# An expert mixture with its unseen first expert in a 64-slot pass, its sorting done ahead of the passes, and its low halves laid over the raw blocks

## The reference, cut to what matters

```python
def swiglu(h, wg, wu, wd):
    return (jax.nn.silu(h @ wg) * (h @ wu)) @ wd

def moe_swiglu(h, router, wg, wu, wd):
    t = h.reshape(B_ * S_, D_)
    logits = (t @ router).astype(jnp.float32)
    top_v, top_i = lax.top_k(logits, TOP_K)
    gates = jax.nn.softmax(top_v, axis=-1)
    gate_full = jnp.sum(jax.nn.one_hot(top_i, N_EXPERTS, dtype=jnp.float32) * gates[..., None], axis=1)
    out = jnp.zeros_like(t)
    for e in range(N_EXPERTS):
        out = out + gate_full[:, e:e + 1].astype(t.dtype) * swiglu(t, wg[e], wu[e], wd[e])
    return out.reshape(B_, S_, D_)
```

## Time and profile before

| | us |
|---|---|
| median of 3 runs | 3103.74 (3100.64 to 3104.61) |
| the profiled execution | 3096.48 |
| its span | 3094.7 |
| TensorE busy | 2879.8 (93%) |
| VectorE busy | 2287.9 (74%) |
| ScalarE busy | 1651.6 (53%) |
| transfers | 739.29 MB, mean 239 GB/s |
| mean granted TensorE clock | 0.969 |

### The profile page before, as it was taken

How to read it: one execution, slowest core, us unless ns; L and a number is a source line. 1 busy time by engine, 2 the same in 40 slices (tenths; PEclk the granted TensorE clock), 3 DMA queues, 4 the chain that set the end, 5 groups by cost and what they waited for, 6 DMA issues and landing times. The chain is left out here.

```text
span 3094.7 us, 49251 instructions
## 1 busy us (share of the span) xinstructions
PE 2879.8 (93%) x17960; PEld 2375.9 (77%) x17961; DVE 2287.9 (74%) x3284; ACT 1651.6 (53%) x1865; POOL 72.3 (2%) x75
## 2 busy tenths in 40 slices
PE   7999898999999999989889988879998998999988
PEld 3796546898888999977769976668877877888776
DVE  5675754889788666666655567668889889888988
ACT  4354303335534344346344354357778778777886
POOL 0000000000000000000000000000000100000010
PEclk9999899999999999999889999879999999999999
DMA  8570232455687666633145331289999999999997
GB/s 310 204 253 30 106 146 91 144 164 186 257 257 238 201 214 210 213 130 127 57 150 183 122 129 38 107 345 373 364 374 419 397 371 419 394 373 379 390 408 284
DMA packets 228491, 739.29 MB, mean 239 GB/s; under 512 B 23831, under 2 KB 60104, under 8 KB 225480
## 3 DMA queue, kind: packets, MB, share of 16 engines
q1 hardware_dynamic: 222648, 704.49, 62.0%
q0 software_dynamic: 5360, 31.98, 3.1%
q10 hardware_dynamic: 288, 0.26, 0.0%
HBM read 707.28 MB, written 29.36 MB: 238 GB/s over the span
## 5 line engine op out<-in xcount | busy, mean ns | idle before, releaser
L3942 DVE TENSOR_TENSOR moe_lo<-moe_raw,moe_hi 128x2048 fp32r<-128x2048 f32 (+1 forms) x397 | 860.0, 2191 | 125.3 <-ACT moe_hi L3745 123.5
L3745 ACT ACTIVATE moe_hi<-moe_raw 128x2048 fp32r<-128x2048 f32 (+1 forms) x397 | 724.0, 1838 | 245.5 <-PE moe_pB L3611 105.2
L3611 PE MATMUL moe_pB<-moe_hi,moe_hEh 128*128 128x512 f32 x560 | 223.9, 400 | 7.0 <-DVE moe_hEl L4121 5.7
L3611 PE MATMUL moe_pB<-moe_lo,moe_hEh 128*128 128x512 f32 x560 | 220.1, 393 | 0.0
L3611 PE MATMUL moe_pB<-moe_hi,moe_hEl 128*128 128x512 f32 x560 | 219.9, 393 | 0.0
L1971 PE MATMUL exp_pO<-exp_vh,exp_ah 128*128 128x512 f32 x512 | 200.1, 391 | 1.8 <-DVE exp_al L2056 1.8
L1971 PE MATMUL exp_pO<-exp_vl,exp_ah 128*128 128x512 f32 x512 | 200.0, 391 | 0.0
L3623 PE MATMUL moe_pB<-moe_hi,moe_hEh 128*128 128x512 f32 x448 | 182.7, 408 | 18.4 <-DVE moe_lo L3942 17.8
L1971 PE MATMUL exp_pO<-exp_vh,exp_al 128*128 128x512 f32 x512 | 199.2, 389 | 0.0
L1996 ACT ACTIVATE exp_vh<-value_ring 128x1024 fp32r<-128x1024 f32 x128 | 134.8, 1056 | 103.4 <-PE exp_pO L1971 81.5
L2045 DVE TENSOR_TENSOR exp_vl<-value_ring,exp_vh 128x1024 fp32r<-128x1024 f32 x128 | 156.4, 1222 | 30.6 <-ACT exp_vh L1996 28.6
(11 more groups left out here) (861 smaller groups left out, 7268.0 us busy)
## 6 DMA issues: line engine op xcount, KB each, us to landing
moe_raw<-in_moe_w SPq DMA_DIRECT2D x758, 512.0 KB, 7.7
value_ring<-in_peer_v SPq DMA_DIRECT2D x128, 512.0 KB, 4.4
key_ring<-in_peer_u SPq DMA_DIRECT2D x64, 512.0 KB, 3.6
exp_us<-in_peer_u SPq DMA_DIRECT2D x64, 512.0 KB, 5.1
inp_w<-in_w_mod SPq DMA_DIRECT2D x48, 512.0 KB, 7.5
inp_w<-in_w_tiles SPq DMA_DIRECT2D x40, 512.0 KB, 6.2
gates<-route_big POOLq DMA_DIRECT2D x8, 2048.0 KB, 7.2
exp_gs<-gates SPq DMA_DIRECT2D x32, 512.0 KB, 5.7
```

What stands on the lines that cost most here:

```text
L3611: i = pe.matmul(pB[:, kind], l[:, kd], m[:, n % HALVES, ns], start=kd == 0 and x == 0, stop=kd == KD - 1 and x == 2)
L3745: act.activation(hi[:, n % HALVES:n % HALVES + count_], raw[:, n % RING:n % RING + count_], ACT.Copy).then_inc(hi_ready, count_)
L3942: dve.tensor_tensor(lo[:, n % HALVES:n % HALVES + count_], raw[:, n % RING:n % RING + count_], hi[:, n % HALVES:n % HALVES + count_], ALU. ...
```

## The change

- WIDE, RANKS: pass 0 becomes narrow. The order is narrow, wide, wide, narrow, wide, narrow, wide, narrow, and the wide passes keep ranks 1 to 4. EXTRA goes from 4 to 5.
- The ring `lo` is gone. The low halves are written over the raw blocks: `low` is a second, fp32r tensor at the address of `raw`, 21 slots. The ring `hi` has HIGH = 12 slots in place of 6 (the sum of the tiles stays 33 blocks).
- A raw slot is loaded again when TensorE has used the block in it (`used`), not when VectorE has lowered it; the first 21 loads wait for nothing.
- The first three conversions (EARLY = 3, six blocks) of ScalarE and VectorE stand ahead of pass 0; in pass 0 ScalarE waits for `used` only from the 13th block on.
- `tables` stands ahead of the counts, `ranks` and `sorted_passes` among the first three low operations; PREPARE of what is left is gates after 5, extras after 9, extra_slots after 15, and a new part, extra_gates (the gates of the extra passes, until now the end of `gates`), after 19. Scratch for the sorting moves to the tile hrow.
- The split of the first tokens is the narrow one, 64 slots a bank.

```diff
-    WIDE = (True, True, False, True, False, True, True, False)
-    RANKS = (0, 1, 5, 2, 6, 3, 4, 7)
-    EXTRA = 4
+    WIDE = (False, True, True, False, True, False, True, False)
+    RANKS = (0, 1, 2, 5, 3, 6, 4, 7)
+    EXTRA = 5
...
-    RING, HALVES, PRE = 21, 6, 2
+    RING, HIGH, PRE, EARLY = 21, 12, 2, 3
...
-        both = n % RING < RING - 1 and n % HALVES < HALVES - 1
+        both = n % RING < RING - 1 and n % HIGH < HIGH - 1
...
+    def first_turn(t):
+        return isinstance(t.at, int) and t.at == 0
...
-        hi, lo = sb("hi", [P, HALVES, D], F32R), sb("lo", [P, HALVES, D], F32R)
+        low = nc.alloc_sbuf_tensor_at("moe_low", [P, RING, D], F32R, offset=nc.sbuf_base - RING * D * 4)
+        hi = sb("hi", [P, HIGH, D], F32R)
...
-        AHEAD_LO, AHEAD_USED = RING, HALVES
+        AHEAD_USED = HIGH
...
-                    sp.wait_ge(lo_ready, t.at * PASS + n + 1)
+                    if not first_turn(t) or n >= RING:
+                        sp.wait_ge(used, t.at * PASS + (n + 1 + HIGH - RING))
                     sp.dma_start(raw[:, n % RING], ...).then_inc(raw_loaded[n % RING], 16)
...
-                    pe.wait_ge(lo_ready, AHEAD_LO + t.at * PASS + n + 1)
+                    pe.wait_ge(lo_ready, t.at * PASS + (n + 1))
...
-                            for x, m in enumerate((hi, lo)):
-                                i = pe.matmul(pB[:, kind], hEh[:, kd], m[:, n % HALVES, ns], ...)
+                            for x, m in enumerate((high_of(n), low[:, n % RING])):
+                                i = pe.matmul(pB[:, kind], hEh[:, kd], m[:, ns], ...)
...
-                    act.wait_ge(used, t.at * PASS + n + count_)
-                    act.activation(hi[:, n % HALVES:n % HALVES + count_], raw[...], ACT.Copy).then_inc(hi_ready, count_)
+                    if not first_turn(t) or n + count_ > HIGH:
+                        act.wait_ge(used, t.at * PASS + (n + count_))
+                    act.activation(hi[:, n % HIGH:n % HIGH + count_], raw[...], ACT.Copy).then_inc(hi_ready, count_)

                 high(fixed[0], SPANS[0])
                 act.wait_ge(d_ready, 1)
                 act.activation(e[:], df[:], ACT.Exp).then_inc(e_ready, 1)
+                for span in SPANS[1:EARLY]:
+                    high(fixed[0], span)
...
-                PREPARE = {4: tables, 6: ranks, 8: sorted_passes, 10: extras, 12: extra_slots, 14: gates}
+                tables()
+                dve.wait_ge(rank_psum, 1)
...
+                def lower(t, span):
+                    n, count_ = span
+                    dve.wait_ge(hi_ready, t.at * PASS + n + count_)
+                    dve.tensor_tensor(low[:, n % RING:n % RING + count_], raw[:, n % RING:n % RING + count_], hi[:, n % HIGH:n % HIGH + count_], ALU.subtract).then_inc(lo_ready, count_)
+
+                lower(fixed[0], SPANS[0])
+                ranks()
+                for span in SPANS[1:EARLY]:
+                    lower(fixed[0], span)
+                sorted_passes()
+
+                PREPARE = {5: gates, 9: extras, 15: extra_slots, 19: extra_gates}
...
-                dve.tensor_tensor(hEl[:, 0:KD // 2]..., pX[:, 0], hEh[:, 0:KD // 2]..., ALU.subtract)
+                for h, ready in enumerate((half_ready, hEh_ready)):
+                    ks = slice(h * KD // 2, (h + 1) * KD // 2)
+                    dve.wait_ge(ready, 1)
+                    i = dve.tensor_tensor(hEh[:, ks, HALF:P], pX[:, h]...[:, :, 0:HALF], hEh[:, ks, 0:HALF], ALU.subtract)
+                i.then_inc(h_ready, 1)
```

More of the change, by code:

```diff
@@ L3609, in wide_product @@
                             ns, kd = slice(b * BANK, (b + 1) * BANK), 2 * u + b
-                            for x, (l, m) in enumerate(((hEh, hi), (hEh, lo), (hEl, hi))):
-                                i = pe.matmul(pB[:, kind], l[:, kd], m[:, n % HALVES, ns], start=kd == 0 and x == 0, stop=kd == KD - 1 and x == 2)
+                            for x, (l, m) in enumerate(((hEh, high_of(n)), (hEh, low[:, n % RING]), (hEl, high_of(n)))):
+                                i = pe.matmul(pB[:, kind], l[:, kd], m[:, ns], start=kd == 0 and x == 0, stop=kd == KD - 1 and x == 2)
                         i.then_inc(used, 1)
@@ L3651, in wide_down @@
                             hs = slice(h * BANK, (h + 1) * BANK)
-                            for x, (l, m) in enumerate(((ah, hi), (ah, lo), (al, hi))):
-                                i = pe.matmul(pY[:, h], l[:, u], m[:, n % HALVES, hs], start=g == 0 and u == 0 and x == 0,
+                            for x, (l, m) in enumerate(((ah, high_of(n)), (ah, low[:, n % RING]), (al, high_of(n)))):
+                                i = pe.matmul(pY[:, h], l[:, u], m[:, hs], start=g == 0 and u == 0 and x == 0,
                                               stop=g == GROUPS - 1 and u == UNITS - 1 and x == 2)
@@ L3664, in narrow_down @@
                             hs = slice(h * BANK, (h + 1) * BANK)
-                            for x, m in enumerate((hi, lo)):
-                                i = pe.matmul(pY[:, h], both[:, u], m[:, n % HALVES, hs], start=g == 0 and u == 0 and x == 0,
+                            for x, m in enumerate((high_of(n), low[:, n % RING])):
+                                i = pe.matmul(pY[:, h], both[:, u], m[:, hs], start=g == 0 and u == 0 and x == 0,
                                               stop=g == GROUPS - 1 and u == UNITS - 1 and x == 1)
@@ L3811, in narrow @@
                             narrow_silu(t, last)
-                        high(t, span)
+                        if s >= EARLY or not first_turn(t):
+                            high(t, span)
                         if s == behind_block(UNITS):
@@ L4020, in gates, with extra_gates @@
                         pick(meta[:, a, 0:NE, 1], gated[:, a])
+                    dve.nop().then_inc(meta_ready, 1)
+                def extra_gates():
+                    over_row = over[:].rearrange("p e j -> p (e j)")
                     for a in range(TT):
@@ L4082, in wide @@
                     for s, span in enumerate(SPANS[1:], 1):
-                        low(t, span)
-                        if isinstance(t.at, int) and t.at == 0 and s in PREPARE:
-                            PREPARE[s]()
+                        lower(t, span)
                         for g in range(GROUPS):
@@ L4097, in narrow @@
                             narrow_product(t, last)
-                        low(t, span)
+                        if s >= EARLY or not first_turn(t):
+                            lower(t, span)
+                        if first_turn(t) and s in PREPARE:
+                            PREPARE[s]()
                         for g in range(last):
```

48 lines of the change are left out of this document (19 added, 29 removed).

## The result

| | before | after |
|---|---|---|
| median, same chip | 3102.65 us (3100.64 to 3104.61) | 3052.55 us (3046.22 to 3061.25) |
| ratio | | 0.984 (0.9811 to 0.9869) |
| profiled execution | 3096.48, span 3094.7 | 3046.22, span 3044.4 |
| end of pass 0 | 2168.0 | 2135.7 |
| from there to the end | 926.7 | 908.7 |

The change takes 50.1 us off the median and 50.3 off the span. The span's 50.3 are 32.3 up to the end of pass 0 (39.5 forecast) and 18.0 behind it (26.2 forecast). Some 1.7 of the 32.3 are not the change's: the stage begins that much earlier in this execution, with the same code ahead of it (its first load at 2002.0 for 2003.8, VectorE's counts at 2009.57 for the 2011.19 of the earlier trace rows).

A forecast was written before the change was run, and what follows sets the result against it. VectorE was taken to bound narrow passes, idled by a six-slot high ring, and TensorE wide ones. Gains of 39.5 and 26.2 made 65.7 us, profiled 3096.5 to 3030.8; median forecast 3038, rounded to 3040, range 3022 to 3074.

The forecast's parts named there:

- Bounds: Expert mixture: TensorE sets wide passes (121 us); VectorE sets narrow ones (107.5), 98.5 of work plus 9.0 idle from six-slot ring.
- Number of passes: Expert passes: expert 0's 20 tokens fit 64 slots, one extra pass before and after, 758 loads, the fifth extra doesn't run.
- Part 1, the start: Start of the expert stage: early conversions beside the gathering let TensorE start at 2023.5, 5.2 us earlier.
- Part 2, pass 0: First expert pass, now narrow: 102.1 us of VectorE work, end at 2128.5; with the earlier start a gain of 39.5.
- rival B: Pass 0: preparation and ordered ScalarE and VectorE waits mesh badly, 15 of the 39.5 us go, 3055 us; chance 10%.
- the wait for the gates' table: Pass 0: TensorE's 6.84 us wait goes, as gates come after VectorE's fifth low operation, not its 14th.
- Part 3, the narrow passes: The four other narrow passes: twelve high slots return 6.5 of 9.0 us idle; 13.0 for two, 13.2 for the last two.
- about 153 blocks: Last two narrow passes: transfers of these blocks plus 2.4 MB at 419 GB/s cap them at 204 us; 205.5 taken.
- Part 4, the ring: Raw slots free only after TensorE's use: 8 landed blocks, a narrow pass eats 6, wide ones refill; costed at nothing.
- Rival C: Raw ring: a slot's round exceeds 26.2 us, at 30 us narrow passes take 120, kernel slower at 3130 us; chance 4%.
- The sum: Whole kernel: gains of 39.5 and 26.2 make 65.7 us, the profiled execution falls from 3096.5 to 3030.8, median forecast 3040.
- The rule weighed: Transfers: the skill's 358 GB/s limit would make a narrow pass 126 us and its gain nothing; rejected for the trace's 419.

The follow-up runs named there:

- e3_high6: The changed kernel with six high slots in place of twelve, low halves still over the raw blocks: 3084.29 us, ratio 0.9949 to the kernel before.
- e1_oldrings: The changed kernel with the old rings, six high and six separate low slots, raw slots reloaded once lowered: 3080.89 us, ratio 0.9936 to the kernel before.
- e6_mesh: The changed kernel with sorted passes before the second low pair, the 1 MB token store behind eight loads, gates after the fourth low operation: 3053.95 us, ratio 0.9842.
- e5_alternate: The changed kernel with narrow and wide passes in turn, without the second index tile a wide last fixed pass needs: 3047.41 us, ratio 0.9828.
- e11_alternate_right: The changed kernel with narrow and wide passes in turn, plus the second index tile and TensorE's bank wait in the extra pass: 3044.06 us, ratio 0.9817.
- e4_extra4: The changed kernel with four possible extra passes in place of five: 3045.59 us, ratio 0.9827 to the kernel before.
- e9_all_right: The changed kernel with alternating passes, second index tile, bank wait, rearranged first-pass list, earlier last conversions in narrow passes and four extras: 3038.40 us, ratio 0.9799.
- e12_ring14: The changed kernel with 14 raw slots in place of 21, all else the same: 3077.28 us, ratio 0.993 to the kernel before.
- e7_ends: The changed kernel with the last hidden high and low halves of every narrow pass one conversion earlier: 3050.48 us, ratio 0.9834 to the kernel before.

## Why the prediction was right, and where its size was off

**Bounds.** Right: narrow passes were VectorE's, and the idle time in them came from six high slots (e3_high6 keeps it with the rest of the change made, e1_oldrings too).

**Number of passes.** Right, 758 loads.

**Part 1, the start.** By the trace's time TensorE started 0.9 later than forecast (2024.44 for 2023.5), but that is luck in part, since the stage began 1.6 earlier. From VectorE's counts on, 2.7 of the 5.2 came and 2.6 are missing. The term was sized with blocks landed when wanted; ScalarE waited 3.53 for one and VectorE 2.82 behind it. The forecast had named that loss, "up to 3 us". e6_mesh, with the store later, needs 11.9 us for this stretch, where the forecast had 12.3.

**Part 2, pass 0.** The failed term is 102.1 of VectorE's work: from 2024.44 to 2135.7 its busy time is 104.69, its idle time 6.6, together 111.3 where the forecast had 105. I took the six blocks lowered early off a narrow pass's work. But every pass begins and ends with VectorE ahead: at 2135.7 it had lowered pass 0's 84 blocks, a pair of pass 1 and a third of the next, 1.3 pairs or 3.0 us that the credit left out. The preparation was as sized (0.4 less). And the idle time: 5.0 for ScalarE, of which one wait of 3.56 is the mesh of rival B, where I had 3.1 in all, at the end. So the 6.1 over are 2.6 of work and 3.5 of waiting. e6_mesh shows the knot can be moved but that most of it then stands elsewhere. With the 0.9 of the start and rounding, the end stands 7.2 late (2135.7 for 2128.5). By its length, which doesn't count where the stage began, pass 0 gained 30.2, and 9.3 of the 39.5 are missing. The wait for the gates' table is gone, as said.

**Part 3, the narrow passes.** Two steps, off in opposite ways. Passes behind a wide one gained 8.2 each (108.1 to 99.9), where I gave 6.5: twice that is 16.4 for 13.0. I had left VectorE 2.5 of idle time; it has 1.6, the 2.6 at the pass end being TensorE's alone. The last two passes gained 5.7 (217.3 to 211.6), where I gave 13.2. The failed step is "about 153 blocks": I let them draw on 15 blocks of stock at 419 GB/s. The first of the two took its 99.9 and with it the stock; moving (99.9 x 406 - 1.2 MB) / 0.524 = 75 blocks it used 84. The second then had a pass's own 45.3 MB to wait for, 111.6 us at 406 GB/s, and measured 111.7. e5_alternate and e11_alternate_right put a wide pass between and get 101.8 and 102.1.

The end behind the last gathering is 3.5 longer (21.7 for 18.2), for which the forecast had no term: it counted 0.2 for a fifth extra pass, in pass 0. TensorE's first output matmuls in before, after and e4_extra4, and their busy time and clock in after:

```profile
3086.81 1.98 PE L3732 MATMUL moe_pB<-moe_y,moe_Pg 128*128 128x512 f32 x4 [1.06 <-DVE moe_y L4131]
3035.05 3.43 PE L3745 MATMUL moe_pB<-moe_y,moe_Pg 128*128 128x512 f32 x4 [2.76 <-DVE moe_y L4155]
3035.52 1.98 PE L3745 MATMUL moe_pB<-moe_y,moe_Pg 128*128 128x512 f32 x4 [3.04 <-DVE moe_y L4155]
3035.05:3038.48 3.43, 3.43 (x5) 1.65 (x6) 0.69 (x1) 0.00 (x0) 0.00 (x0) 0.57 0.00 0
```

They start 12.3 us behind the gathering where they started after 10.3: 2.1 later, of which 1.3 are the fifth empty turn (e4_extra4) and 0.8 stay unexplained. And all eight take 5.1 in place of 3.7, the first four 3.43 at a granted clock of 0.57, mostly 1.2 GHz, in place of 1.98 at 1.00. That is the other 1.4. The clock is not shown to belong to the change: e6_mesh and e11_alternate_right, with the same code for the end, took 1.98 there and had ends of 20.2 and 20.3, while e9_all_right with four extras had a clock of 0.55 over all eight and an end of 21.9. Nor does it go with the starved pass ahead: e4_extra4 has one and a clock of 1.00 over these matmuls, and e9 has none (ScalarE waits 1.8 for loads in its extra pass).

**Part 4, the ring.** "Just enough" was right for one narrow pass at a time and was then forgotten in part 3, where the same sum (78 moved, 84 used, 6 of 8 eaten) forbids a second. e12_ring14 shows it from the other side. Rival C's round of 26.2 us never decided: it would have cost all passes in e12_ring14, and cost only the narrow ones.

**The sum.** By lengths, 30.2 + 16.4 + 5.7 - 3.5, less 0.3 of wide passes, is 48.5 of the stage; the other 1.8 of the span's 50.3 is where the stage began. Missing from 65.7 are 9.3 in pass 0, 7.5 in the last two passes, 3.5 at the end and the 0.3; 3.4 came unforeseen. That leaves 17.2, of which the early begin hides 1.8.

**The rule weighed.** The trace of after holds 414 GB/s over 115 us of pass 0, and its passes of 99.9 us exist. The figure of about 358 GB/s in the Trainium skill (DMA: Bandwidth & Descriptors, Specifications) doesn't hold for this core, which runs alone. Its page HBM Reference (Specifications (TRN2)) gives a core alone some 425 GB/s, and with that the traces agree: no stretch shown here has more than 420.

## What to carry to other kernels

Where one kind of pass consumes faster than the transfers deliver and another slower, the ring is a stock: reckon per pass what is moved and what is used, in sequence, and put the slow kind between the fast ones. A buffer's depth is found by the wait that ends at its slot, and only the ring with that wait is worth deepening. Work done ahead of a pipelined pass saves only the part by which it exceeds the lead that every pass hands to the next.

## What the runs showed of the hardware that was not expected

GpSimd adds two numbers of one element ahead of each fetch of rows. In before and then in after, the timeline of a narrow pass:

```profile
2348.06 0.18 POOL L3878 TENSOR_TENSOR moe_hold<-moe_hold 1x1 f32<-1x1 f32 x1 [53.12 <-DVE moe_gidx L4071]
```

```profile
2431.18 13.51 POOL L3895 TENSOR_TENSOR moe_hold<-moe_hold 1x1 f32<-1x1 f32 x1 [50.55 <-DVE moe_gidx L4094]
```

(The profile's spans on GpSimd are rough.) It takes 0.18 us at each of its nine places in before, e1_oldrings and e3_high6, whose narrow passes leave VectorE idle 9 us, and about 13.5 in the narrow passes of 99.9 us of every other kernel, where VectorE's two-operand subtractions stand back to back (the POOL column: 4.08 in the earlier trace rows, 17.55 above). In the starved extra passes behind a narrow one it takes 2.1. e12_ring14, starved by transfers, has 20.8 us over its nine, 13.5 of them in pass 0, where the kernels with passes of 99.9 have 43 and more. In a narrow pass 0 it is 0.2 in some kernels and 13.5 in others. This is a correlation, no run isolates the cause. It cost nothing here, the rows being wanted some 24 us later. The Trainium skill (GPSIMD Engine Reference, the row on SBUF interfaces) says that GpSimd contends with VectorE instructions that take two inputs from SBUF; the traces fit that, with 13.5 us for an operation of one element beside subtractions of 2.29, but don't show it.

A wait of 2.6 us at a narrow pass's end can cost more than itself: at 19 of 33 such ends the granted clock was 0.86 or less and the wide pass behind took 121.9 to 123.4, while with a wait of 0.4 it was 1.00 at eleven of eleven and the pass took 120.2, once 120.7 (e7_ends).
